# First norm in chunks, modulation on TensorE in column strips, interleaved with the first projection

## The chip, the cores and the metric

The kernel runs on one core of a Trainium2 chip. The time is the device time of one execution in microseconds. The kernel before took 2334.73 us (median of 3 runs, 2334.53 to 2340.07).

## The reference

Two blocks follow each other on 512 tokens with 1024 features, in f32. The first has two layers with a modulated norm. It also carries 256 context tokens through its first layer:

```python
sc, scc = silu(c), silu(c_ctx)
mod = split(sc @ w_mod[l] + b_mod[l], 6)       # shift1, scale1, gate1, shift2, scale2, gate2
mod_c = split(scc @ w_mod[l] + b_mod[l], 6)    # the same for the context
hn = rms_norm(h, g_norm1[l]) * (1 + mod_c[1]) + mod_c[0]
xn = rms_norm(x, g_norm1[l]) * (1 + scale1) + shift1
p = xn @ w_in[l]    # queries, keys, values; Fourier, convolution and pool inputs
```

Attention, a Fourier mixer, a convolution of width 31 with a layer norm, and a pool mixer work on p; an output projection and a SwiGLU follow. The second block has a retention layer with a short convolution and an attention layer with latent projections. The change touches only the first layer of the first block, up to its mixers.

## The kernel before

Features lie on the 128 partitions in eight chunks, tokens along the free axis: 512 of x and 256 of the context side by side, 768 in the first layer. x stays in X (`resid`) for the whole kernel.

Every large product is cut into panels of 128 output features (`panel`, L530). A panel's weights (512 KB) come into a ring of four slots. ScalarE writes their high part (`high`, L977), and VectorE (`panel_low`, L1393) or GpSimd (L523) the low part. The operand is split in the same way, and a panel step, one chunk k of the contraction, is six matmuls: high by high, low by high and high by low, each on 512 and 256 tokens. The first projection, win0, has 13 panels; `big` runs twelve one after the other, and the last stands among the mixers.

SyncE issues all loads of the ring in one written order (`ring_order`, L86). A load waits until its slot's content four places earlier has been used: a panel by `lo_ready`, a modulation block by `shift_used` or `mod_step`. The first 16 places hold the modulation blocks of shift1 (0 to 7) and scale1 (8 to 15), taken in turn. They come ahead of the first panel; x is loaded as one transfer behind the first two of them.

The shift blocks go to TensorE (L838): w is stationary and silu(c) is moving, with two columns, one for x and one for the context. The scale blocks go to VectorE (`ring_mod`, L1476; `modulate`, L1468): for each of the two vectors one multiply-and-sum pass over 128x1024. Five more blocks are done the same way right behind the first norm (L1669 to L1674), seven among the mixers (`behind`, L1761), the others later.

The first norm: ScalarE squares a chunk (L1009), GpSimd adds it to a running sum (L504). TensorE sums over partitions (L582), ScalarE takes the root (L1018), VectorE inverts (L1383) and TensorE spreads the result to all partitions (L595). For each chunk VectorE forms t = x * a * r (L1435) and ScalarE adds the shift to give the high part (L1034). The low part is VectorE's for even chunks (L1423) and GpSimd's for odd ones (L510). Panel 0 takes each chunk as it becomes ready.

In the projection VectorE makes the low parts of panels 2 to 12, the gated product for the convolution, norms and rotations of q and k, and the 62 taps of the convolution (L1684), with a table of how many have to be done at which point. The mixers (`mixers`) run ten attention pairs with other steps in between, by the table BETWEEN. The step `mean` in pair 4 sums the convolution over features on TensorE (L732) and waits for all 62 taps.

## Time and profile before

| | us |
|---|---|
| median of 3 runs | 2334.73 |
| the profiled execution | 2335.68 |
| its span | 2333.6 |
| TensorE busy (PE) | 2191.2 |
| VectorE busy (DVE) | 1211.2 |
| ScalarE busy (ACT) | 725.2 |
| GpSimd busy (POOL) | 652.0 |

Busy times come from the page's first part. PE is a matmul, PEld a load of stationary weights, and the two overlap. L544 is the line that holds every panel matmul, so where it is in time is told by the timeline. An f32 matmul outside the panels appears as two instructions, one for each of its passes. A row of the timeline merges neighbours of the same kind: start, length, engine and line, output and input, shape, count, and in brackets how long the engine stood idle before and what released it.

### The profile page before, as it was taken

The page shows a single profiled execution, that of the slowest core. Times are in us where ns is not written, and L with a number is a line of the kernel's source. Part 1 is how long each engine was busy: PE and PEld are TensorE (multiplying, and loading weights), DVE is VectorE, ACT ScalarE, POOL GpSimd, SP SyncE. Part 2 cuts the span into 40 slices and gives each one's busy share as a digit, 9 for nine tenths or more (in the row PEclk, how much of TensorE's full clock was granted, in tenths as well). Part 3 has the DMA queues.
Part 4 walks back from the last instruction along what each step waited for, and adds up shares of the span by engine and source line. Part 5 has one row for each costly group of instructions (what it writes and reads, how often), then busy time and mean ns, then how long its engine had stood idle before and what let it go on. Part 6 is the DMA issues. An engine that isn't in the chain of part 4 may idle for free.

```text
span 2333.6 us, 26283 instructions
## 1 busy us (share of the span) xinstructions
PE 2191.2 (94%) x10898; PEld 1764.2 (76%) x10898; DVE 1211.2 (52%) x1548; ACT 725.2 (31%) x1073; POOL 652.0 (28%) x283
## 2 busy tenths in 40 slices
PE   5898897999999999799989999998999999899997
PEld 5785576888888888685568888876778888778655
DVE  5996577566555665587454302346332344432265
ACT  2323433222112221424542212223253222234542
POOL 2100002223332233200044434433224444423302
PEclk9999998999999999899999999999999999989998
DMA  7312132334333333121023323322223333212301
GB/s 262 122 46 90 37 136 64 108 127 137 111 105 125 122 129 113 59 73 73 1 86 100 111 79 93 113 83 82 81 64 89 92 100 100 90 46 58 101 1 54
DMA packets 60165, 213.57 MB, mean 92 GB/s; under 512 B 6672, under 2 KB 10384, under 8 KB 59792
## 3 DMA queue, kind: packets, MB, share of 16 engines
q1 hardware_dynamic: 57888, 206.92, 27.6%
q10 hardware_dynamic: 2160, 4.98, 0.6%
q8 instruction: 87, 1.43, 0.3%
q14 instruction: 30, 0.25, 0.0%
HBM read 209.77 MB, written 2.10 MB: 91 GB/s over the span
## 4 chain that ended last, share of the span: by engine, by line
PE 85%; DVE 8%; ACT 3%; issue 2%; DMA 1%; POOL 1%; SPq 0%; ACTq 0%; DVEq 0%
PE prod L544 73%; PE misc L582 2%; PE prod L719 1%; PE prod L687 1%; DMA ring<-in_wmod 1%; PE prod L595 1%; PE prod L774 1%; ACT operand_hi L1034 1%; PE misc L903 1%; PE misc L647 1%; PE misc L798 1%; PE prod L624 1%; DVE work L1435 1%; PE misc L786 1%; DVE operand_lo L1407 1%
## 5 line engine op out<-in xcount | busy, mean ns | idle before, releaser
L523 POOL TENSOR_TENSOR wlo<-ring,whi 128x1024 fp32r<-128x1024 f32 (+3 forms) x256 | 610.4, 2385 | 1591.5 <-ACT whi L981 1591.5
L544 PE MATMUL prod<-operand_hi,whi 128*128 128x512 f32 (+1 forms) x2208 | 735.4, 373 | 36.2 <-DVE operand_lo L1423 14.1
L544 PE MATMUL prod<-operand_hi,wlo 128*128 128x512 f32 (+1 forms) x2208 | 725.1, 368 | 0.0
L544 PE MATMUL prod<-operand_lo,whi 128*128 128x512 f32 (+1 forms) x2208 | 721.3, 367 | 0.0
L981 ACT ACTIVATE whi<-ring 128x1024 fp32r<-128x1024 f32 (+3 forms) x284 | 293.5, 1034 | 736.5 <-PE prod L544 736.5
L544 PEld LDWEIGHTS prod<-operand_hi,whi 128*128 128x128 f32 x2208 | 381.8, 190 | 127.9 <-issue 28.2
L544 PEld LDWEIGHTS prod<-operand_hi,wlo 128*128 128x128 f32 x2208 | 380.6, 190 | 68.7
L544 PEld LDWEIGHTS prod<-operand_lo,whi 128*128 128x128 f32 x2208 | 379.4, 190 | 69.4 <-issue 2.4
L1473 DVE CUSTOM_DVE_ANT_0 mod_junk<-modw,silu_c,par 128x1024 bf16<-128x1024 f32 x68 | 123.7, 1820 | 79.2 <-DMA modw<-in_wmod 78.6
L544 PE MATMUL prod<-hidden_hi,whi 128*128 128x512 f32 (+1 forms) x528 | 160.6, 358 | 0.0
L544 PE MATMUL prod<-hidden_lo,whi 128*128 128x512 f32 (+1 forms) x528 | 160.4, 358 | 0.0
L544 PE MATMUL prod<-hidden_hi,wlo 128*128 128x512 f32 (+1 forms) x528 | 160.4, 358 | 0.0
L1502 DVE SCALAR_TENSOR_TENSOR resid<-prod,par,resid 128x512 f32<-128x512 f32 x72 | 45.4, 659 | 183.3 <-PE prod L544 183.2
L1799 DVE TENSOR_TENSOR hidden_lo<-ffn_h,hidden_hi 128x768 fp32r<-128x768 f32 (+1 forms) x44 | 112.5, 2556 | 42.6 <-ACT hidden_hi L1231 42.6
L1796 DVE TENSOR_TENSOR ffn_h<-ffn_silu,prod 128x768 f32<-128x768 f32 (+1 forms) x44 | 36.1, 821 | 188.0 <-PE prod L544 188.0
L1473 DVE CUSTOM_DVE_ANT_0 modw<-modw,silu_c,par 128x1024 f32<-128x1024 f32 x68 | 132.5, 1948 | 0.0
L1684 DVE SCALAR_TENSOR_TENSOR conv_acc<-glu,par,conv_acc 128x798 f32<-128x798 f32 (+1 forms) x120 | 104.4, 913 | 1.3
L1226 ACT ACTIVATE ffn_silu<-prod 128x768 f32<-128x768 f32 (+1 forms) x44 | 31.1, 706 | 224.4 <-PE prod L544 224.4
L544 PEld LDWEIGHTS prod<-hidden_hi,whi 128*128 128x128 f32 x528 | 87.1, 188 | 16.6 <-POOL wlo L523 0.5
L544 PEld LDWEIGHTS prod<-hidden_lo,whi 128*128 128x128 f32 x528 | 87.1, 188 | 16.1
L544 PEld LDWEIGHTS prod<-hidden_hi,wlo 128*128 128x128 f32 x528 | 87.1, 188 | 16.1
L1156 ACT ACTIVATE probs_t<-misc 128x512 f32<-128x512 f32 x52 | 31.0, 595 | 73.7 <-PE misc L786 73.7
(244 smaller groups left out, 2173.8 us busy)
## 6 DMA issues: line engine op xcount, KB each, us to landing
ring<-in_w SPq DMA_DIRECT2D x224, 512.0 KB, 3.6
modw<-in_wmod SPq DMA_DIRECT2D x68, 512.0 KB, 3.7
ring<-in_w SPq DMA_DIRECT2D x32, 704.0 KB, 4.9
ring<-in_wmod SPq DMA_DIRECT2D x28, 512.0 KB, 4.7
dft<-in_dftx SPq DMA_DIRECT2D x8, 512.0 KB, 5.2
resid<-in_xt SPq DMA_DIRECT2D x1, 3072.0 KB, 13.7
ring<-in_w SPq DMA_DIRECT2D x12, 192.0 KB, 2.3
ret_r<-in_decay ACTq DMA_DIRECT2D x8, 256.0 KB, 2.9
```

The lines of the kernel that those rows point to most:

```text
L523: nc.gpsimd.tensor_tensor(wlo[j % 2][:, 0:w], ring[PLACE["panel", j] % RING][:, 0:w], whi[j % 2][:, 0:w].bitcast(F32), ALU.subtract).then_ ...
L544: mm = pe.matmul(G[b][:, t0:t0 + tn], w[v][:, k * P:(k + 1) * P], a[:, t0:t0 + tn], start=(i == 0 and q == 0), stop=(i == g.kc - 1 and q = ...
L582: mm = pe.matmul(out[:, h * tb:h * tb + h], square[:, t:t + P], sel, start=(c == 0 and tb == 0), stop=(c == nchunks - 1 and tb == nb - 1), ...
L595: mm = pe.transpose(M0[:, tb * P:(tb + 1) * P], r[:, tb * P:(tb + 1) * P], ident)
L981: nc.scalar.activation(whi[j % 2][:, 0:w], ring[PLACE["panel", j] % RING][:, 0:w], ACT.Copy).then_inc(hi_ready, 1)
L1156: nc.scalar.activation(probs_t[at % 3][:, :], M1[:, :], ACT.Copy).then_inc(pair_copied, 1)
L1226: nc.scalar.activation(fsilu[:, 0:width], src[:, 0:width], ACT.Silu).then_inc(free, 1)
L1473: nc.vector.tensor_tensor_reduce((junk, w)[s][:, 0:DC * P], w[:, 0:DC * P], silu_c[:, 1024 * s:1024 * (s + 1)], 1.0, col, ALU.mult, ALU.ad ...
L1502: ins = nc.vector.scalar_tensor_tensor(X[:, p, t0:t0 + tn], G[b][:, t0:t0 + tn], pa(f"mod{l}")[:, col:col + 1], X[:, p, t0:t0 + tn], ALU.m ...
L1684: ins = nc.vector.scalar_tensor_tensor(o, glu[:, c, tap:tap + wide], w, o, ALU.mult, ALU.add)
L1796: nc.vector.tensor_tensor(fh[:, 0:width], fsilu[:, 0:width], G[b][:, 0:width], ALU.mult).then_inc(bank_free[b], 1)
L1799: nc.vector.tensor_tensor(HL[:, p // 2, 0:width], fh[:, 0:width], HH[:, p // 2, 0:width].bitcast(F32), ALU.subtract).then_inc(h_lo, 1)
```

## The change

- Parameters, constants and x come first. Constants are issued on ScalarE's queue, x in four transfers with a semaphore each; c for VectorE's products comes behind the load of panel 3.
- ScalarE squares each chunk as its quarter lands; VectorE adds the squares instead of GpSimd.
- All 16 blocks of shift1 and scale1 go to TensorE, with silu(c) as the stationary operand, padded with zeros from 2 to 32 columns, and w as the moving one. The eight contraction chunks of a block go in turn to four column strips of 32, so that eight matmuls leave four partial sums in rows 0 to 127. ScalarE copies the rows of a chunk out (`mod_copy`), and TensorE multiplies them with a 0/1 matrix (`pick`), which adds the four partial sums and puts features back on partitions. VectorE adds the bias and forms the factor for that chunk alone (`mod_chunk`) ahead of its t.
- On TensorE the sum of squares comes first, then the chunks of modulation, from chunk 4 on between the steps of panels 0 and 1. These two run side by side, panel 1 one step behind. Modulation runs four chunks ahead.
- On ScalarE the high parts of panels 0 and 1 stand ahead of the copies of chunks 1 and 2.
- The ring holds six blocks, panels 0 and 1, ten blocks, panels 2 and 3, and then blocks 16 to 20 in turn with panels 4 to 8.
- Blocks 16 to 20 are multiplied on VectorE between the low parts of panels 2 to 7 instead of behind the norm. Fifty instead of 62 convolution taps lie in the projection; the other twelve stand in pairs 0, 2, 3 and 4 of the mixers (`beside`).

The buffers for the padded vector and the copied rows lie in space that is free then; new semaphores are declared. The diff without these:

```diff
-MOD_PE = 8
-MOD_FIRST = 16
+MOD_PE = 16
...
     panels = [("panel", j) for g in GEMMS for j in range(g.j0, g.j0 + g.n)]
-    first = [("mod", k // 2 + MOD_PE * (1 - k % 2)) for k in range(MOD_FIRST)]
-    order = first + panels[:2]
-    for i in range(4):
-        order += [("mod", MOD_FIRST + k) for k in ((0, 1), (2,), (3,), (4,))[i]] + [panels[2 + i]]
+    first = [("mod", k // 2 + DC * (1 - k % 2)) for k in range(MOD_PE)]
+    order = first[:6] + panels[:2] + first[6:] + panels[2:4]
+    for i in range(5):
+        order += [("mod", MOD_PE + i), panels[4 + i]]
     cut = GEMM["wout0"].j0 + 2
-    return order + panels[6:cut] + [("mod", k) for k in range(MOD_FIRST + 5, MOD_RING)] + panels[cut:]
+    return order + panels[9:cut] + [("mod", k) for k in range(MOD_PE + 5, MOD_RING)] + panels[cut:]
...
     for name, w in (("ident", 128), ("ones", 128), ("perm1", 128), ("perm2", 128), ("mask", 128),
-                    ("invw", 2), ("edge", 32), ("inv", 1), ("eps", 1), ("half", 2)):
+                    ("invw", 2), ("edge", 32), ("inv", 1), ("eps", 1), ("half", 2), ("pick", 2)):
...
         def _(sp):
-            sp.dma_start(silu_c[:, :], d["c"]).then_inc(c_landed, 16)
             sp.dma_start(par[:, :], d["par"]).then_inc(par_landed, 16)
-            sp.dma_start(con[:, :], d["con"]).then_inc(par_landed, 16)
+            for s in range(4):
+                sp.dma_start(X[:, 2 * s:2 * s + 2, :], d["xt"][:, 2 * s:2 * s + 2, :]).then_inc(x_landed[s], 16)
...
                 elif i < MOD_PE:
-                    sp.wait_ge(shift_used, i + 1)
+                    sp.wait_ge(shift_used, 2 * (i % DC) + 2 - i // DC)
...
-            for r in range(RING // 2):
-                load_mod(ORDER[r][1])
-            sp.dma_start(X[:, :, :], d["xt"]).then_inc(x_landed, 16)
             own = MOD_RING
-            for kind, j in ORDER[RING // 2:]:
+            for kind, j in ORDER:
...
                 load_panel(j)
+                if j == 3:
+                    sp.dma_start(silu_c[:, :], d["c"]).then_inc(c_landed, 16)
...
         def _(pool):
-            for c in range(1, DC):
-                pool.wait_ge(square_ready, c + 1)
-                wait(pool, square_added, c - 1)
-                nc.gpsimd.tensor_tensor(W[1][:, :], W[1][:, :], W[0][:, :], ALU.add).then_inc(square_added, 1)
             def odd_lows(name):
...
-            pe.wait_ge(c_ready, 1)
-            for k in range(MOD_PE):
-                landed(pe, ("mod", k))
-                w = ring[PLACE["mod", k] % RING]
-                for c in range(DC):
-                    mm = pe.matmul(M0[:, 2 * k:2 * k + 2], w[:, c * P:(c + 1) * P], silu_cp[:, 2 * c:2 * c + 2],
-                                   start=(c == 0), stop=(c == DC - 1))
-                mm.then_inc(shift_used, 1)
+            def modulate(c):
+                bank = (M1, MM)[c % 2]
+                wait(pe, mod_read, c - 1)
+                for q in (1, 0):
+                    landed(pe, ("mod", DC * q + c))
+                    w = ring[PLACE["mod", DC * q + c] % RING]
+                    for i in range(DC):
+                        g = 32 * (i % 4)
+                        mm = pe.matmul(bank[g:g + 32, P * q:P * q + P], silu_cp[:, 32 * i:32 * i + 32], w[:, i * P:(i + 1) * P],
+                                       start=(i < 4), stop=(i >= 4))
+                    mm.then_inc(shift_used, 1)
+            def pick(c):
+                pe.wait_ge(mod_copied, c + 1)
+                for q in range(2):
+                    mm = pe.matmul((M1, MM)[c % 2][:, 256 + 2 * q:258 + 2 * q], mod_rows[c % 2][:, P * q:P * q + P], co("pick"),
+                                   start=True, stop=True)
+                mm.then_inc(mod_picked, 1)
+            def first_panels(p, k):
+                def ready(k):
+                    if k % 2:
+                        pe.wait_ge(odd_lo, k // 2 + 1)
+                    else:
+                        pe.wait_ge(operand_lo, k + 1)
+                panel("win0", p, xh, xl, NT, k, k + 1, ready=ready)
+            pe.wait_ge(con_landed, 16)
+            sum_squares(1, NT, W, total=W[1], out=F[:, 0:8])
+            pe.wait_ge(pad_ready, 1)
+            modulate(0)
+            modulate(1)
+            pick(0)
+            spread_roots(NT, W)
+            modulate(2)
+            pick(1)
+            modulate(3)
+            pick(2)
+            for k in range(DC + 1):
+                if k < DC:
+                    first_panels(0, k)
+                if k + 3 < DC:
+                    pick(k + 3)
+                if k:
+                    first_panels(1, k - 1)
+                if k + 4 < DC:
+                    modulate(k + 4)
...
                 width, segs = tok(l)
-                if l == 0:
-                    rms(1, NT, W, free=lambda: pe.wait_ge(shift_read, 1), total=W[1])
-                else:
+                if l == 1:
...
-                big(f"win{l}", xh, xl, lambda p, l=l: win_width(l, p), ready=OPS[f"win{l}"], after=qk_norm, panels=12)
+                big(f"win{l}", xh, xl, lambda p, l=l: win_width(l, p), ready=OPS[f"win{l}"], after=qk_norm, panels=12,
+                    begin=0 if l else 2)
...
+            def mod_copy(c):
+                act.wait_ge(shift_used, 2 * c + 2)
+                wait(act, mod_picked, c - 1)
+                nc.scalar.activation(mod_rows[c % 2][:, :], (M1, MM)[c % 2][:, 0:256], ACT.Copy).then_inc(mod_copied, 1)
             def norm_mod(l, which, width):
-                root(width, 1024)
-                if l == 0 and which == 0:
+                first = l == 0 and which == 0
+                root(width, 1024, source=F[:, 0:8] if first else None)
+                if first:
+                    mod_copy(0)
                     high(0)
+                    mod_copy(1)
                     high(1)
+                    mod_copy(2)
...
+                    if first and 0 < c < DC - 2:
+                        mod_copy(c + 2)
...
-            act.wait_ge(par_landed, 32)
-            nc.scalar.activation(silu_cp[:, :], pa("c"), ACT.Silu)
-            act.wait_ge(c_landed, 16)
-            nc.scalar.activation(silu_c[:, :], silu_c[:, :], ACT.Silu).then_inc(c_ready, 1)
-            act.wait_ge(x_landed, 16)
+            act.dma_start(con[:, :], d["con"]).then_inc(con_landed, 16)
+            act.wait_ge(par_landed, 16)
+            act.wait_ge(pad_cleared, 1)
+            nc.scalar.activation(silu_cp[:, :].rearrange("p (c s) -> p c s", c=DC)[:, :, 0:2],
+                                 pa("c").rearrange("p (c s) -> p c s", c=DC), ACT.Silu).then_inc(pad_ready, 1)
+            for c in range(DC):
+                act.wait_ge(x_landed[c // 2], 16)
+                wait(act, square_added, c - 2)
+                nc.scalar.activation((W[4 + c % 2] if c else W[1])[:, :], X[:, c, 0:NT], ACT.Square).then_inc(square_ready, 1)
+            n["added"] += DC - 1
+            n["sq"] += 1
+            act.wait_ge(con_landed, 16)
...
                 width, segs = tok(l)
-                if l == 0:
-                    for c in range(DC):
-                        square(c, X[:, c, 0:NT], NT, W[0], W[1], lambda c: None)
                 norm_mod(l, 0, NT)
...
                 def qk_norm(p, l=l):
+                    if l == 0 and p == 1:
+                        act.wait_ge(c_landed, 16)
+                        nc.scalar.activation(silu_c[:, :], silu_c[:, :], ACT.Silu).then_inc(c_ready, 1)
...
-            def norm_mod(l, which, width):
+            def mod_chunk(c):
+                both = pa("mod0")[:, 0:4 * DC].rearrange("p (b c s) -> p c b s", b=2, c=DC)[:, c]
+                dve.wait_ge(mod_picked, c + 1)
+                nc.vector.tensor_tensor(both, both, (M1, MM)[c % 2][:, 256:260].rearrange("p (b s) -> p b s", b=2),
+                                        ALU.add).then_inc(mod_read, 1)
+                dve.wait_ge(mod_read, c + 1)
+                link(nc.vector.tensor_scalar(afac[:, c:c + DC + 1:DC], both[:, 1], 1.0, pa("g10")[:, c:c + 1], ALU.add, ALU.mult))
+            def norm_mod(l, which, width, before=None):
...
                 for c in range(DC):
+                    if before is not None:
+                        before(c)
...
-            dve.wait_ge(par_landed, 32)
-            dve.wait_ge(c_ready, 1)
-            for k in range(MOD_PE, MOD_FIRST):
-                ring_mod(k)
-            dve.wait_ge(shift_used, MOD_PE)
-            shift = pa("mod0")[:, 0:2 * MOD_PE]
-            nc.vector.tensor_tensor(shift, shift, M0[:, 0:2 * MOD_PE], ALU.add).then_inc(shift_read, 1)
-            dve.wait_ge(shift_read, 1)
-            dve.wait_ge(mod_step, mods_done(MOD_FIRST - 1))
+            nc.vector.memset(silu_cp[:, :], 0.0).then_inc(pad_cleared, 1)
+            dve.wait_ge(par_landed, 16)
+            for c in range(1, DC):
+                dve.wait_ge(square_ready, c + 1)
+                wait(dve, square_added, c - 1)
+                nc.vector.tensor_tensor(W[1][:, :], W[1][:, :], W[4 + c % 2][:, :], ALU.add).then_inc(square_added, 1)
...
             n["added"] += DC - 1
-            modulation(0, 0)
-            dve.wait_ge(x_landed, 16)
+            for s in range(4):
+                dve.wait_ge(x_landed[s], 16)
...
                 width, segs = tok(l)
-                norm_mod(l, 0, NT)
+                norm_mod(l, 0, NT, mod_chunk if l == 0 else None)
...
                 link(ins)
-                if l == 0:
-                    for k in range(MOD_FIRST, MOD_FIRST + 3):
-                        ring_mod(k)
                 panel_low(g.j0 + 2)
-                if l == 0:
-                    for k in range(MOD_FIRST + 3, MOD_FIRST + 5):
-                        ring_mod(k)
                 dwa, dwba, ticks = PAR[f"dw{l}"][0], PAR[f"dwb{l}"][0], {}
...
                     panel_low(g.j0 + 3 + 2 * c)
-                    conv_taps(((7, 20), (5, 12))[l][c])
+                    if l == 0 and c == 0:
+                        dve.wait_ge(c_ready, 1)
+                    if l == 0:
+                        ring_mod(MOD_PE + 2 * c)
+                    conv_taps(((5, 16), (5, 12))[l][c])
                     panel_low(g.j0 + 4 + 2 * c)
-                    conv_taps(((13, 26), (10, 18))[l][c])
+                    if l == 0:
+                        ring_mod(MOD_PE + 2 * c + 1)
+                    conv_taps(((9, 21), (10, 18))[l][c])
...
                     panel_low(g.j0 + p + 2)
+                    if l == 0 and p == 5:
+                        ring_mod(MOD_PE + 4)
...
                         rope(PR[:, p - 5, 0:NX], W[4][:, 0:NX])
-                    conv_taps(((33, 39, 45, 51, 57, 62), (25, 35, 45, 53, 57, 62))[l][p - 5])
+                    conv_taps(((25, 30, 35, 40, 45, 50), (25, 35, 45, 53, 57, 62))[l][p - 5])
...
                         pooling(c, part)
+                    if l == 0 and i < 5:
+                        conv_taps((52, 52, 54, 58, 62)[i])
...
                     if l == 0 and i in (0, 3, 4, 5, 6, 7, 8):
-                        ring_mod(MOD_FIRST + 5 + (0, 3, 4, 5, 6, 7, 8).index(i))
+                        ring_mod(MOD_PE + 5 + (0, 3, 4, 5, 6, 7, 8).index(i))
...
     put("eps", EPS)
+    put("pick", i[:, None] % 32 == np.arange(2)[None, :])
...
```

## Rows read from the trace of the kernel before

**Rows 1.** The page, part 1, the whole span: busy us, share, instructions.

```profile
PE 2191.2 (94%) x10898; PEld 1764.2 (76%) x10898; DVE 1211.2 (52%) x1548; ACT 725.2 (31%) x1073; POOL 652.0 (28%) x283
```

**Rows 2.** Windows: stretch, its length, each engine's busy us (x instructions), granted clock, DMA.

```profile
0.00:61.23 61.23, 32.35 (x146) 31.49 (x147) 35.42 (x44) 16.43 (x21) 18.30 (x13) 1.00 0.72 259
61.23:84.69 23.46, 20.14 (x88) 16.43 (x89) 22.72 (x46) 12.71 (x22) 7.80 (x4) 0.93 0.44 134
84.69:182.68 97.99, 97.99 (x578) 84.58 (x576) 90.67 (x105) 21.86 (x28) 0.00 (x0) 1.00 0.20 62
```

**Rows 3.** The chain of waits in the start: start us, length us, what.

```profile
44.60 6.98 PE prod L838 x32
```

**Rows 4.** Timeline of TensorE from the sum of squares into panel 0.

```profile
51.44 2.70 PE L582 MATMUL misc<-con,work 128*128 128x1 f32 x12
55.41 1.54 PE L595 MATMUL prod<-con,work 128*128 128x128 f32 x6 [1.27 <-DVE work L1384]
61.23 0.98 PE L544 MATMUL prod<-operand_hi,whi 128*128 128x512 f32 x2 [4.28 <-DVE operand_lo L1423]
...
63.32 1.01 PE L544 MATMUL prod<-operand_hi,whi 128*128 128x512 f32 x2
...
79.74 0.51 PE L544 MATMUL prod<-operand_hi,whi 128*128 128x512 f32 x2
...
80.80 0.51 PE L544 MATMUL prod<-operand_hi,whi 128*128 128x512 f32 x2
```

**Rows 5.** DMA up to 17.16 us: packets and rate; then KB each, us to landing.

```profile
DMA packets 955, 6.20 MB, mean 361 GB/s; under 512 B 96, under 2 KB 224, under 8 KB 699
...
resid<-in_xt SPq DMA_DIRECT2D x1, 3072.0 KB, 13.7
```

**Rows 6.** DMA up to 100 us, one modulation block of the ring.

```profile
ring<-in_wmod SPq DMA_DIRECT2D x21, 512.0 KB, 4.6
```

**Rows 7.** Timeline of all engines: first squares, operands of panel 0, behind panel 0.

```profile
17.16 1.58 ACT L1009 ACTIVATE work<-resid 128x768 f32<-128x768 f32 x2 [7.86 <-DMA resid<-in_xt]
...
51.62 0.17 DVE L1647 TENSOR_TENSOR par<-par,prod 128x16 f32<-128x16 f32 x1 [3.18 <-PE prod L838]
...
56.99 2.19 DVE L1435 SCALAR_TENSOR_TENSOR work<-resid,afac,prod 128x512 f32<-128x512 f32 x4 [1.63 <-PE prod L595]
58.17 2.17 ACT L1034 ACTIVATE operand_hi<-work,par 128x512 fp32r<-128x512 f32 x4 [1.83 <-DVE work L1435]
59.32 1.76 DVE L1423 SCALAR_TENSOR_TENSOR operand_lo<-work,par,operand_hi 128x512 fp32r<-128x512 f32 x2
...
61.43 1.84 POOL L510 TENSOR_TENSOR operand_lo<-work,operand_hi 128x768 fp32r<-128x768 f32 x1 [1.28 <-ACT work L1034]
...
76.29 0.81 ACT L1181 ACTIVATE conv_acc<-prod 128x768 f32<-128x768 f32 x1 [2.50 <-PE prod L544]
...
77.00 1.05 ACT L981 ACTIVATE whi<-ring 128x1024 fp32r<-128x1024 f32 x1
...
81.16 1.22 DVE L1397 TENSOR_TENSOR wlo<-ring,whi 128x1024 fp32r<-128x1024 f32 x1
```

**Rows 8.** Groups of instructions by shape, VectorE's adds of squares: count | busy, mean ns.

```profile
L1375 DVE TENSOR_TENSOR work<-work,work 128x768 f32<-128x768 f32 x7 | 6.7, 954 | 1.0 <-ACT work L1009 1.0
```

**Rows 9.** Timeline, one weighing of V, two strips of 64 columns, two narrow windows.

```profile
218.97 0.39 PE L798 MATMUL misc<-probs_t,vtok 128*64 128x128 f32 x4
...
219.08 0.28 PE L798 MATMUL misc<-probs_t,vtok 128*64 128x128 f32 x2
```

**Rows 10.** Timeline of VectorE: taps in the projection, mixers.

```profile
92.77 6.48 DVE L1684 SCALAR_TENSOR_TENSOR conv_acc<-glu,par,conv_acc 128x798 f32<-128x798 f32 x6
...
207.94 1.28 DVE L1473 CUSTOM_DVE_ANT_0 mod_junk<-ring,silu_c,par 128x1024 bf16<-128x1024 f32 x1 [12.14 <-issue]
...
250.64 0.68 DVE L1407 TENSOR_TENSOR operand_lo<-misc,operand_hi 128x512 fp32r<-128x512 f32 x1
```

**Rows 11.** Timeline of TensorE in pair 4: the layer norm's mean.

```profile
252.05 2.95 PE L732 MATMUL prod<-conv_acc,con 128*128 128x512 f32 x8
```

9 lines of the change are left out of this document (6 added, 3 removed).

## The prediction

> **What bounds the kernel now.** I read the page's busy times first: TensorE is busy for 94% of the span [rows 1], so a gain has to come from the places where it stands still or runs slowly. The windows show where one lies. Up to 61.23 us TensorE is busy for 32.35 us, none of it on a projection, and from 61.23 to 84.69 for 20.14 of 23.46 us. From 84.69 to 182.68 it is busy for all 97.99 us [rows 2]. Panel 1 of the first projection ends at 84.69, so everything ahead of that point is the start. The chain of waits names what holds the start: the last two shift blocks on TensorE end at 51.6 us [rows 3], behind 16 block loads of which eight wait for VectorE's two multiply-and-sum passes. Only then come the sum of squares (2.70 us), the spread of the roots (1.54 us) and, at 61.23 us, the first projection matmul [rows 4]. A step of a panel (six matmuls) starts every 2.09 us there and every 1.06 us from 79.74 us on [rows 4]: TensorE's lower (1.2 GHz) and its upper level (2.4 GHz).
>
> **What goes, comes and moves.** I time the new start on TensorE up to the point that answers to 84.69 us.
>
> *Squares.* Parameters and constants (0.6 MB by their widths) and x (3072 KB, [rows 5]) now come first, 3.7 MB. In the first 17.16 us 6.20 MB came in, 361 GB/s on average [rows 5], so the last quarter of x lands near 11 us instead of 17. A square takes ScalarE some 0.84 us for a chunk [rows 7] and an add on VectorE 0.95 us [rows 8]; the seven adds run behind the landings and end near 14.0 us (bounds 13 and 16). GpSimd's adds go. Sum of squares, at the lower level, 2.7 us: 16.8 us.
>
> *Modulation of one chunk.* Two blocks, each eight matmuls with 32 stationary and 128 moving columns in f32, that is two passes each, 32 passes a chunk. No row has four strips. The nearest is the weighing of V in two strips of 64 columns: two passes start inside each 0.11 us at the upper level (four passes from 218.97, the last two from 219.08) [rows 9]. Four strips at once would be 8 slots of 0.11, 0.9 us a chunk. No overlap would be 32 passes, 3.5 us. Two at a time, as in the row, would be 1.8. I take 1.3 us, between four and two at a time, and twice that, 2.6 us, at the lower level. The Trainium skill (TensorE: Matmul & The Clock Gate, Part 3, "The mechanism") says that a weight load overlaps running matmuls only where the row groups differ, and here all strips use all rows. By that rule each load would stand between matmuls and a chunk would cost at least the 3.5 us. The two strips of this trace share all rows too and do run together, so I keep this as a rival.
>
> *Pick.* Four passes against 128-column weights at 0.225 us (2.70 us for 12 in rows 4): 0.9 us low, 0.4 high. The ACT copy ahead of it, 128x256, is a third of a chunk's high part (2.17 us for two chunks, [rows 7]), so under 0.5 us, and lies beside the next chunk's matmuls. It costs nothing while that next chunk is there; without cover it would be 0.5 us for each.
>
> *Order on TensorE.* Chunks 0 and 1, pick, spread: 16.8 + 5.2 + 0.9 + 1.5 = 24.4 us. Chunk 2: 27.0. The blocks of chunk 3 may load only as chunk 2's ring slots come free, the second at 27.0, and a load takes 4.6 us [rows 6]: its last half starts at 31.6, chunk 3 ends at 32.9, pick 2 at 33.8. By then panels 0 and 1 have landed and been split (their loads start near 21 us, and high parts stand ahead of the copies on ScalarE), and VectorE and ScalarE have chunks 0 and 1 ready: t takes VectorE 1.1 us a chunk, the high part ScalarE 1.1, the low part 1.2 to 1.8 [rows 7]. The new wait for a pick stands ahead of each t on VectorE; behind it wait t, then ScalarE's high part, then GpSimd's odd low part. Its two tiny instructions are near the 0.17 us of the shift add [rows 7], 0.45 us a chunk with the handshake. Four steps pass: k=0 still low, 2.1 + 0.9 + 2.6 = 5.6 us; k=1 to 3 high, two panel steps, pick and chunk, 2.1 + 0.4 + 1.3 = 3.8 us each. That is 50.8 us. VectorE and ScalarE need about 2.2 us a chunk for operands and are ahead. Step k=4 and pick 7 end at 52.3. From there chunk 7's own chain ends last: 0.45 + 1.1 + 2.2 (ScalarE writes high part and a copy) + 1.84 (GpSimd's low part) = 5.6 us, then three panel steps, 3.2 us: 61.1 us.
>
> *Panel 2.* Before, its low part lay ready while panel 1 ran for 8.5 us. Now panel 1 ends 2.1 us after panel 0, and sigmoid 0.81, high part 1.05 and low part 1.22 [rows 7] take 3.1 us: a new stall of 1.0 us. Panel 2 starts at 62.1 instead of 84.69. **Gain of the start: 22.6 us.**
>
> *VectorE behind it.* Five block products (two passes of 1.28 us, [rows 10]) leave the end of the start and go between panels 2 to 7; twelve conv taps of 1.08 us (6.48 us for six, [rows 10]) leave the projection for the mixers. The sums are equal (12.8 and 13.0 us) and VectorE is busy 90.67 of 97.99 us there [rows 2], with an earlier beginning now, so TensorE stays covered; for a low part that comes a little late at panel 6 or 7 I put 0.5 us (0 to 5). Two of the twelve taps stand before the 12.14 us wait for a modulation load [rows 10] and cost nothing. Two and four in front of pairs 3 and 4's norms shift these by some 1.3 us, which a running TensorE hides. The last four do not hide: they start when VectorE has finished a low part at 250.64 + 0.68 = 251.32 us [rows 10] and end at 255.65, while TensorE now starts the layer norm's mean, which needs all taps, at 252.05 [rows 11]. **Loss: 3.6 us** (0 if TensorE has a reserve there, 5 if the shift before it adds up). The silu of c moves behind panel 1's evacuation, where ScalarE is busy 21.86 of 97.99 us [rows 2]: nothing.
>
> *Sum.* -22.6 + 0.5 + 3.6 = -18.5 us. The profiled execution took 2335.68 us (span 2333.6), so 2317.2; it lies 0.95 us above the median of 2334.73, so the forecast is **2316 us**.
>
> **The rivals.**
> 1. *Strips run in full parallel and the mean's wait is hidden.* A chunk at 0.9/1.8 us brings panel 2 to 58 us or so, and the 3.6 us stay out: 2309 us. For it: the two strips of rows 9 overlap completely. Against: weight loads of four strips in 0.11 us are seen nowhere. 0.20.
> 2. *TensorE stays at its lower level through the interleaved steps.* k=1 to 3 then cost 4.2 + 0.9 + 2.6 = 7.7 us each and the end 4.6 us more, panel 2 starts near 78.4: 2335.7 - 6.3 + 4.1, by the median 2332 us. For it: before 61 us TensorE ran its block matmuls seven us without a gap and its sum of squares still at 0.225 us a pass [rows 3, 4]. Against: the same trace is at the upper level by 79.74, with the steps that now make half of the mix. 0.12.
> 3. *Slower: strips one after another.* Place: TensorE's modulation; price 3.5 us a chunk high and 7.0 low. Chunk 3 then ends at 23.8 + 24.5 = 48.3, the steps at 77.2 and panel 2 starts at 88.5, 3.8 later than now, with the mixers' 4.1: 2343 us, and with the clock low throughout 2365. It decides from 5.7 us for a cold chunk (each extra us there counts six times: 3.5 chunks ahead, one in k=0, three halves). That is where the skill's rule on weight loads leads. Rows 9 speak against it. 0.08.
> 4. *VectorE becomes the bound of the projection.* With 5 more us of late low parts there and 1 or 2 in the mixers: 2323 us. For it: 93% busy in rows 2, and a product that waits for its block holds every low part behind it. Against: the sum of its work doesn't grow. 0.10.
>
> **How the numbers follow.** My forecast, 2311 to 2323 in itself, has 0.50. Differences within 0.3% (7 us) can't be told from none. Faster: the forecast, rivals 1 and 4, 0.80. Same: rival 2, 0.12. Slower: rival 3, 0.08. The range goes from rival 1 to just under rival 2: 2308 to 2331 us, which leaves out about 0.2.
>
> **What would show it.** Right: first projection matmul near 34 us; panel 2's first near 62; four modulation passes started in some 0.15 us at the upper level; squares' last add at 14 us; TensorE without a gap from panel 2 to the mixers; the wait before the mean (line 732's instructions) named after conv taps, about 3.6 us. Wrong: a modulation chunk over 3.2 us, matmuls of panel steps still 0.43 us apart after 45 us, loads for chunks 3 to 7 landing after the previous step has ended, or low parts of panels 4 to 8 named as what TensorE waits for.

## The result

| | median, us | runs | ratio to before |
|---|---|---|---|
| kernel before | 2334.73 (2334.53 to 2340.22) | 5 | |
| changed kernel | 2319.53 (2315.53 to 2321.93) | 5 | 0.9924 [0.9908, 0.9941] |

The change made the kernel 15.2 us faster by the medians. The forecast was 2316 us, 3.5 us lower, and its range (2308 to 2331) held the time. The profiled execution of the changed kernel took 2319.09 us, its span 2317.3 us.

### The profile page after: what moved, and what is told of

Read it like the earlier page. It is cut to its first block, busy times and chain, and to the rows that moved or that the text cites. A ratio compares the mean times of both kernels' runs of the same rounds, so it can differ in the third digit from the quotient of the medians.

```text
span 2317.3 us, 26618 instructions
## 1 busy us (share of the span) xinstructions
PE 2182.1 (94%) x11058; PEld 1753.8 (76%) x11058; DVE 1189.9 (51%) x1537; ACT 730.3 (32%) x1083; POOL 637.0 (27%) x276
## 4 chain that ended last, share of the span: by engine, by line
PE 86%; DVE 7%; ACT 3%; issue 1%; DMA 1%; POOL 1%; SPq 0%; ACTq 0%; DVEq 0%
PE prod L542 74%; PE misc L580 2%; PE prod L717 1%; PE prod L685 1%; PE prod L772 1%; DMA ring<-in_wmod 1%; DVE conv_acc L1742 1%; PE misc L941 1%; PE misc L645 1%; PE prod L593 1%; PE misc L796 1%; PE prod L622 1%; PE misc L784 1%; DVE operand_lo L1463 1%; PE misc L613 1%
## 5 line engine op out<-in xcount | busy, mean ns | idle before, releaser
L1742 DVE SCALAR_TENSOR_TENSOR conv_acc<-glu,par,conv_acc 128x798 f32<-128x798 f32 (+1 forms) x120 | 104.6, 914 | 1.3
L542 PEld LDWEIGHTS prod<-hidden_hi,whi 128*128 128x128 f32 x528 | 87.2, 188 | 16.3 <-POOL wlo L521 0.5
```

The source lines that it names most:

```text
L542: mm = pe.matmul(G[b][:, t0:t0 + tn], w[v][:, k * P:(k + 1) * P], a[:, t0:t0 + tn], start=(i == 0 and q == 0), stop=(i == g.kc - 1 and q = ...
L1742: ins = nc.vector.scalar_tensor_tensor(o, glu[:, c, tap:tap + wide], w, o, ALU.mult, ALU.add)
```

## The profile after

The page's first part, engine by engine: busy us, share of the span, instructions. It answers to [rows 1].

```profile
PE 2182.1 (94%) x11058; PEld 1753.8 (76%) x11058; DVE 1189.9 (51%) x1537; ACT 730.3 (32%) x1083; POOL 637.0 (27%) x276
```

TensorE's busy time fell by 9.1 us while the span fell by 16.3: part of the gain is work that ran at the higher clock level or went away, the rest is standing time.

The windows of the changed kernel, in the columns of [rows 2]. I cut at events: first panel matmul, panel 2's first, the end of attention's first scores, the mean, the last scores of layer 0.

```profile
0.00:34.57 34.57, 13.25 (x158) 10.77 (x159) 13.51 (x21) 15.88 (x24) 5.07 (x7) 0.86 0.76 276
34.57:62.25 27.68, 26.16 (x244) 21.82 (x244) 15.17 (x44) 14.96 (x27) 7.17 (x4) 0.92 0.80 295
...
157.75:231.38 73.63, 59.10 (x329) 37.75 (x329) 47.34 (x88) 29.53 (x60) 4.75 (x2) 0.92 0.22 79
231.38:281.19 49.81, 41.74 (x217) 26.32 (x218) 29.97 (x55) 23.92 (x36) 0.00 (x0) 0.84 0.17 48
```

The same cuts in the kernel before, by its own events:

```profile
86.10:182.61 96.51, 96.51 (x569) 83.29 (x567) 90.50 (x103) 21.86 (x28) 0.00 (x0) 1.00 0.19 58
182.61:252.05 69.44, 58.58 (x329) 37.47 (x328) 36.25 (x77) 28.78 (x59) 4.76 (x2) 0.95 0.23 84
252.05:297.66 45.61, 37.53 (x220) 23.57 (x218) 29.98 (x55) 24.68 (x38) 0.00 (x0) 0.93 0.17 52
```

Laid side by side, in us:

| stretch | before | after | difference |
|---|---|---|---|
| start to panel 2's first matmul | 86.10 | 62.25 | -23.85 |
| panel 2 to the first scores | 96.51 | 95.50 | -1.0 |
| first scores to the mean | 69.44 | 73.63 | +4.2 |
| mean to the last scores of layer 0 | 45.61 | 49.81 | +4.2 |
| everything behind | 2036.0 | 2036.1 | +0.1 |
| span | 2333.6 | 2317.3 | -16.3 |

So the start gained 23.85 us and the mixers gave back 8.4. In the fourth row TensorE is *busy* 4.2 us longer with the same matmuls, and the granted clock is 0.84 where it was 0.93: that half of the loss is no standing time at all.

The timeline of TensorE in the changed kernel shows the start and the two places in the mixers (start, length, what, and in brackets the idle time before and its releaser):

```profile
15.79 2.69 PE L580 MATMUL prod<-con,work 128*128 128x1 f32 x12 [15.79 <-DVE work L1713]
18.41 3.54 PE L840 MATMUL misc<-ring,silu_c_by_feature 128*32 128x128 f32 x64
...
25.97 1.08 PE L840 MATMUL misc<-ring,silu_c_by_feature 128*32 128x128 f32 x16 [1.87 <-DMA ring<-in_wmod]
...
28.72 1.01 PE L848 MATMUL misc<-con,mod_rows 128*128 128x2 f32 x4 [1.68 <-ACT mod_rows L1063]
...
31.36 2.22 PE L840 MATMUL misc<-ring,silu_c_by_feature 128*32 128x128 f32 x32 [1.62 <-DMA ring<-in_wmod]
...
34.57 0.98 PE L542 MATMUL prod<-operand_hi,whi 128*128 128x512 f32 x2
...
39.06 0.62 PE L542 MATMUL prod<-operand_hi,whi 128*128 128x512 f32 x2
...
41.80 1.08 PE L840 MATMUL misc<-ring,silu_c_by_feature 128*32 128x128 f32 x32
...
62.25 0.61 PE L542 MATMUL prod<-operand_hi,whi 128*128 128x512 f32 x2 [1.06 <-DVE wlo L1453]
...
231.38 5.58 PE L730 MATMUL prod<-conv_acc,con 128*128 128x512 f32 x8 [3.56 <-DVE conv_acc L1742]
...
247.96 5.28 PE L580 MATMUL prod<-con,glu 128*128 128x1 f32 x24
```

Three things are to be seen. A modulation chunk (32 passes, L840) takes 1.08 us at the upper level (41.80). At the lower one it takes 1.77 us where two stand in a row (half of 3.54, 18.41) and 2.22 us behind a wait (31.36). Ahead of the first panel matmul TensorE waits 1.87 + 1.68 + 1.62 = 5.2 us for blocks and for one copy. And the mean's eight matmuls, 2.95 us in [rows 11], take 5.58 behind the 3.56 us wait for the taps; the 24 passes of the next sum of squares, 17 us later, take 5.28. In the kernel before they take 3.71:

```profile
265.56 3.71 PE L582 MATMUL prod<-con,glu 128*128 128x1 f32 x24
```

That is 2.63 + 1.57 = 4.2 us, the whole of the table's fourth row. The two parts are of different kinds. The mean runs at the upper level in the kernel before. The sum of squares is in part at the lower level there too: the windows of these 24 passes, before and after, have a granted clock (the number behind the five engines) of 0.74 and 0.50.

```profile
265.56:269.13 3.57, 3.57 (x27) 3.57 (x25) 0.00 (x0) 0.00 (x0) 0.00 (x0) 0.74 0.02 5
```
```profile
247.96:253.10 5.14, 5.14 (x27) 5.14 (x25) 0.00 (x0) 0.00 (x0) 0.00 (x0) 0.50 0.02 3
```

VectorE and ScalarE in the changed kernel, start and mixers, where the adds, squares and late taps are:

```profile
9.38 6.27 DVE L1713 TENSOR_TENSOR work<-work,work 128x768 f32<-128x768 f32 x6 [0.23 <-ACT work L1219]
...
6.51 1.57 ACT L1219 ACTIVATE work<-resid 128x768 f32<-128x768 f32 x2 [1.91 <-DMA resid<-in_xt]
...
13.62 0.84 ACT L1219 ACTIVATE work<-resid 128x768 f32<-128x768 f32 x1 [0.22 <-DVE work L1713]
...
226.93 4.30 DVE L1742 SCALAR_TENSOR_TENSOR conv_acc<-glu,par,conv_acc 128x798 f32<-128x798 f32 x4
```

The adds end at 15.65. The last square (13.62) waits for an add and not for x. The four taps before the mean are one solid row: 1.08 us each with nothing between, as in [rows 10].

## Experiments

Eleven kernels ran, each an edit of the changed kernel. The line labels in the rows are those of each kernel. Landmarks from the traces, in us:

| kernel | first panel matmul | panel 2 | first scores | mean starts | its 8 matmuls | last scores |
|---|---|---|---|---|---|---|
| before | 61.23 | 86.10 | 182.61 | 252.05 | 2.95 | 297.66 |
| changed | 34.57 | 62.25 | 157.75 | 231.38 | 5.58 | 281.19 |
| e1 | 34.12 | 61.97 | 158.10 | 229.66 | 4.61 | 278.13 |
| e2 | 34.00 | 61.82 | 161.96 | 231.59 | 2.95 | 277.19 |
| e3 | 40.32 | 71.33 | 166.82 | 238.87 | 5.01 | 287.82 |
| e4 | 40.76 | 78.23 | 174.36 | 247.60 | 5.59 | 297.42 |
| e5 | 39.11 | 68.75 | 164.24 | 237.28 | 5.35 | 286.76 |
| e6 | 50.68 | 70.90 | 167.04 | 240.88 | 5.66 | 290.78 |
| e7 | 39.15 | 66.88 | 162.38 | 236.04 | 5.59 | 285.86 |
| e8 | 35.98 | 65.88 | 162.02 | 234.97 | 5.24 | 284.27 |
| e9 | 34.01 | 61.43 | 156.93 | 219.38 | 2.95 | 266.54 |
| e10 | 34.25 | 64.00 | 160.13 | 233.00 | 2.95 | 278.59 |
| e11 | 34.84 | 62.29 | 157.79 | 222.61 | 4.64 | 271.13 |

What lies behind the last scores (the start of layer 0's last two score matmuls) takes 2031.8 to 2039.5 us from trace to trace, though only e9 and e11 change anything there, the places of a few block products. Landmarks are therefore compared with landmarks, times with times. The kernel before had a median of 2333.85 us beside e1 to e4, 2337.19 beside e5 to e8 and 2336.0 beside e9 to e11; ratios are to these.

### e1_taps_pair0: the twelve late taps in front of the wait for a block

```diff
-                        conv_taps((52, 52, 54, 58, 62)[i])
+                        conv_taps((60, 60, 60, 60, 62)[i])
```

> The changed kernel with ten of the twelve moved taps in pair 0, where VectorE stands still for its modulation block, two in pair 4, none in pairs 2 and 3. Theory W (the taps ahead of the mean cost the wait and TensorE's clock behind it): the 3.6 us wait of the mean falls to under 2 us, the mean's matmuls take 2.95 us again instead of 5.58 and the 24 passes of the norm's squares 3.7 instead of 5.3; 5 to 8 us off, a time of 2311 to 2314 us. Rival F (the wait only takes the place of a later one): the wait goes, but under 2 us come off, 2318 us or more.

2317.10 us, ratio 0.9925 [0.9907, 0.9944]. The timeline of TensorE:

```profile
229.66 4.61 PE L730 MATMUL prod<-conv_acc,con 128*128 128x512 f32 x8 [1.38 <-DVE conv_acc L1742]
```

The wait shrank from 3.56 to 1.38 us, but the matmuls behind it still ran slow, and the mean to the last scores took 48.47 us against 49.81. So theory W was right on the wait and wrong on the clock: 2.95 us had been expected for the mean, and 5 to 8 us off. The landmark came 3.1 us earlier; in the time nothing can be told from the changed kernel's 0.9924.

### e2_taps_projection: all 62 taps in the projection again

```diff
-                    conv_taps(((5, 16), (5, 12))[l][c])
+                    conv_taps(((7, 20), (5, 12))[l][c])
-                    conv_taps(((9, 21), (10, 18))[l][c])
+                    conv_taps(((13, 26), (10, 18))[l][c])
-                    conv_taps(((25, 30, 35, 40, 45, 50), ...)[l][p - 5])
+                    conv_taps(((33, 39, 45, 51, 57, 62), ...)[l][p - 5])
-                        conv_taps((52, 52, 54, 58, 62)[i])
+                        conv_taps(62)
```

> All 62 taps in the projection again, with the five block products beside them. Theory V (VectorE has 7 us of room there, 88.4 busy of 95.5 us): 13 us more taps overrun it by 6 us or so, TensorE waits for low parts or norms of q and k, the mean's wait and its low clock go (8 us); 2315 to 2321 us, with the gain of one eaten by the other. Rival: VectorE's idle time there absorbs them, 2311 us.

2316.04 us, ratio 0.9919 [0.9898, 0.994]. The timeline of TensorE, then the window of the projection:

```profile
109.32 0.87 PE L593 MATMUL prod<-con,work 128*128 128x128 f32 x6 [2.48 <-DVE work L1440]
...
111.13 0.84 PE L542 MATMUL prod<-operand_hi,wlo 128*128 128x512 f32 x2
...
231.59 2.95 PE L730 MATMUL prod<-conv_acc,con 128*128 128x512 f32 x8
...
245.10 3.79 PE L580 MATMUL prod<-con,glu 128*128 128x1 f32 x24
```

```profile
61.82:161.96 100.14, 97.65 (x566) 84.44 (x566) 97.79 (x118) 25.30 (x31) 0.00 (x0) 0.98 0.25 74
```

With no wait ahead of the mean both rows are back, at 2.95 and 3.79 us, and the stretch from the mean to the last scores is 45.6 us, as before. Here VectorE is what the projection waits for: it is busy 97.79 of the projection's 100.14 us, and that stretch is 4.6 us longer than with fifty taps. TensorE stands 2.5 us for the inverted roots (L593), and the two panel steps behind this wait take 1.83 and 1.90 us instead of 1.06, with panel matmuls at the lower level (0.84 us for two at 111.13). From the first scores to the last scores e2 takes 115.2 us against 123.4. So the twelve taps cost some 8 us behind the projection or 4.6 inside it, but the last scores come only 4.0 us sooner, and the times don't differ measurably. The result lies in the range that theory V gave.

### e3_pool_adds: the adds of squares on GpSimd

```diff
-            for c in range(1, DC):                 # VectorE
-                ...
-                nc.vector.tensor_tensor(W[1], W[1], W[4 + c % 2], ALU.add)
+            for c in range(1, DC):                 # GpSimd
+                ...
+                nc.gpsimd.tensor_tensor(W[1], W[1], W[4 + c % 2], ALU.add)
```

> The seven adds of squares on GpSimd again, all else as changed. Theory P (the sum of squares stands at the head of the path): an add with its handshake takes 2.76 us instead of 1.06, the last ends near 27 instead of 15.7, panel 2 starts 8 to 11 us later, 2328 to 2331 us. Rival D (block loads set the start, the sum is hidden): under 3 us more.

2324.78 us, ratio 0.996 [0.9945, 0.9975]. The timeline of GpSimd and TensorE:

```profile
8.18 13.47 POOL L507 TENSOR_TENSOR work<-work,work 128x768 f32<-128x768 f32 x7 [7.74 <-ACT work L1224]
...
21.80 2.69 PE L585 MATMUL prod<-con,work 128*128 128x1 f32 x12 [21.80 <-POOL work L507]
...
45.82 0.84 PE L547 MATMUL prod<-operand_lo,whi 128*128 128x512 f32 x2
```

An add takes GpSimd 13.47 / 7 = 1.92 us against 1.05 on VectorE. The sum of squares starts 6.0 us later, panel 2 9.1: the other 3 us are panel steps that are still at the lower level at 45.82 (0.84 us for two matmuls; 0.62 at 39.06 in the changed kernel). The adds are on the path, and having them on VectorE is worth 5 us by the medians, 8 by the ratios. Panel 2's delay lies in the 8 to 11 us of theory P; the time lies 3 us below what it gave.

### e4_one_strip: the same modulation in one column strip

```diff
-                        g = 32 * (i % 4)
+                        g = 0
-                                       start=(i < 4), stop=(i >= 4))
+                                       start=(i == 0), stop=(i == DC - 1))
```

with the copy and the pick on rows 0 to 31 alone.

> All eight matmuls of a modulation block in the same 32 columns, summed in PSUM; the copy and the pick take 32 rows. Theory S (four strips run at once): a chunk costs 3.5 us high and 7 low instead of 0.95 and 1.75; panel 2 starts 20 to 29 us later, 2339 to 2349 us. Rival (the loads of weights, not the matmuls, set a chunk's time): under 5 us more, 2324 us or less.

2332.95 us, ratio 0.9989 [0.9974, 1.0004]. The timeline of TensorE:

```profile
18.35 10.06 PE L840 MATMUL misc<-ring,silu_c_by_feature 128*32 128x128 f32 x64
...
49.19 3.68 PE L840 MATMUL misc<-ring,silu_c_by_feature 128*32 128x128 f32 x32
```

The same 32 passes cost 3.68 us in one strip and 1.08 in four, a factor of 3.4. By the Trainium skill (TensorE: Matmul & The Clock Gate, Part 3, "The mechanism") a weight load overlaps running matmuls only where the row groups differ; all four strips use all rows, and yet they overlap. Without the strips nearly the whole gain is gone. It is a smaller loss than the third rival had, and than the 20 to 29 us that theory S had expected here, since panel 2 comes 16.0 us later: the solid matmuls of the first two chunks take 10.06 us and not 14, so they reached the upper level on their way.

### e5_x_whole: x as one transfer

```diff
-            for s in range(4):
-                sp.dma_start(X[:, 2*s:2*s+2, :], d["xt"][:, 2*s:2*s+2, :]).then_inc(x_landed[s], 16)
+            sp.dma_start(X[:, :, :], d["xt"]).then_inc(x_landed[0], 16)
```

> The changed kernel with x in one transfer. Theory P (the squares stand at the head of the path): the squares start near 11.5 instead of 6.5, the last add ends near 20 instead of 15.7, panel 2 starts 3 to 4.5 us later: 3 to 4.5 us longer than the changed kernel. Rival D (loads of blocks set the start): under 1 us longer.

2323.35 us, ratio 0.9943 [0.9928, 0.9958]. The timeline of ScalarE and VectorE:

```profile
11.75 2.31 ACT L1218 ACTIVATE work<-resid 128x768 f32<-128x768 f32 x3 [7.30 <-DMA resid<-in_xt]
...
13.43 7.33 DVE L1712 TENSOR_TENSOR work<-work,work 128x768 f32<-128x768 f32 x7 [12.30 <-ACT work L1218]
```

The squares begin at 11.75 instead of 6.51, the adds end at 20.76 instead of 15.65, and panel 2 comes 6.5 us later, where 3 to 4.5 had been expected. By medians and by ratios the quarters are worth about 4 us, but the two intervals overlap; the landmarks show the difference, the times alone do not.

### e6_modulation_first: all chunks of modulation ahead of the panels

```diff
+            for k in range(4, DC):
+                modulate(k)
+                pick(k - 1)
+            pick(DC - 1)
             for k in range(DC + 1):
-                if k + 3 < DC:
-                    pick(k + 3)
-                if k + 4 < DC:
-                    modulate(k + 4)
```

> All eight chunks of modulation on TensorE first, then the steps of panels 0 and 1 side by side. Theory I (lying among the panel steps hides the modulation's loads): TensorE waits for the blocks of chunks 4 to 7, all picked near 46 us, then 16 steps of 1.05 us; panel 2 starts near 65 instead of 62.3, 3 us longer than the changed kernel. Rival (chunk 7's chain ends last in either order): within 1 us.

2325.18 us, ratio 0.9949 [0.9931, 0.9967]. The timeline of TensorE:

```profile
47.94 1.08 PE L840 MATMUL misc<-ring,silu_c_by_feature 128*32 128x128 f32 x16 [0.88 <-DMA ring<-in_wmod]
...
50.68 0.99 PE L542 MATMUL prod<-operand_hi,whi 128*128 128x512 f32 x2
```

Chunks 4 and 7 wait for their blocks, four times and 4.3 us in all, and the passes between stay at the lower level: 16 in 1.08 us. Panel 2 comes 8.65 us later; I had put it at 3. So panel steps between the chunks do fill the time of the loads. How much of the 8.65 us is these waits and how much the lower level, this run doesn't part.

### e7_ring_eight_copies_first and e8_copies_first: ring order, and copies ahead of high parts

```diff
-    order = first[:6] + panels[:2] + first[6:] + panels[2:4]
+    order = first[:8] + panels[:2] + first[8:] + panels[2:4]        # e7 only
```
```diff
                     mod_copy(0)
-                    high(0)
                     mod_copy(1)
-                    high(1)
                     mod_copy(2)
+                    high(0)
+                    high(1)                                          # e7 and e8
```

> Eight blocks in the ring ahead of panels 0 and 1 instead of six, and the copies of chunks 0 to 2 ahead of the high parts. Theory L (in the changed kernel TensorE waits for the second blocks of chunks 2 and 3 and for a copy behind a high part, 5.2 us in all): the waits for chunk 3 and for copy 1 go, but panel 0's split now ends last; first projection matmul between 34 and 36 us, against 34.6: within 2 us of the changed kernel. Rival: the splits of panels 0 and 1 have reserve, and 2 to 4 us come off.

> The copies of chunks 0 to 2 ahead of the high parts of panels 0 and 1, all else as changed. Theory L: the 1.7 us wait for copy 1 behind high part 0 goes, but the blocks of chunk 3 land no sooner, so the first projection matmul stays within 0.5 us of 34.6 and the time within 1 us of the changed kernel. Rival: pick 1 comes 1.7 us sooner, and so does everything behind it, 1.5 us off.

e7: 2321.25 us, ratio 0.9932 [0.9915, 0.995]. e8: 2319.89 us, ratio 0.993 [0.991, 0.995]. The timeline of TensorE in e7:

```profile
39.15 0.98 PE L542 MATMUL prod<-operand_hi,whi 128*128 128x512 f32 x2 [9.71 <-DVE operand_lo L1488]
```

and in e8:

```profile
23.48 0.64 PE L840 MATMUL misc<-ring,silu_c_by_feature 128*32 128x128 f32 x16 [0.46 <-DMA ring<-in_wmod]
...
31.67 2.23 PE L840 MATMUL misc<-ring,silu_c_by_feature 128*32 128x128 f32 x32 [5.06 <-DMA ring<-in_wmod]
...
35.98 0.98 PE L542 MATMUL prod<-operand_hi,whi 128*128 128x512 f32 x2 [1.13 <-DVE operand_lo L1488]
...
41.48 0.84 PE L542 MATMUL prod<-operand_lo,whi 128*128 128x512 f32 x2
```

With the panels two places later in the ring, e7's first panel matmul waits 9.7 us and comes at 39.15, not between 34 and 36 as expected. In e8 TensorE waits 5.06 us for chunk 3's block in one piece, where the changed kernel waits 1.62 at that place and 1.7 for a copy earlier, so what the earlier copies save there is lost again to the load. Ahead of the wait e8 is at the upper level (16 passes in 0.64 us at 23.48; the changed kernel is too at that point), behind it at the lower one (32 in 2.23), and its panel steps still are at 41.48. Its first panel matmul comes 1.4 us later, where within 0.5 had been expected, and panel 2 is 3.6 us later. Neither time can be told from the changed kernel's: the order of copies and high parts, and the two places in the ring, were not shown to matter.

### e9_no_product_in_pair0: no block product ahead of pair 1

The longest wait in the changed kernel's mixers is not the mean's. Its waits between 157 and 232 us (what waits <- for what: us, times, longest):

```profile
PE misc L784 <- DVE work L1687: 7.2, 1, 7.2
```

L784 turns a pair's probabilities, which needs a norm of VectorE's; VectorE stands in pair 0's block product. The kernel before waits 12.14 us there ([rows 10]), for nothing that the row names; the changed kernel's timeline names the block's load:

```profile
183.18 1.28 DVE L1540 CUSTOM_DVE_ANT_0 mod_junk<-ring,silu_c,par 128x1024 bf16<-128x1024 f32 x1 [10.06 <-DMA ring<-in_wmod]
```

The kernel before has that product there too, and TensorE waits 7.1 us behind it.

```diff
-                        conv_taps((52, 52, 54, 58, 62)[i])
+                        conv_taps((57, 59, 60, 62, 62)[i])
-                    if l == 0 and i in (0, 3, 4, 5, 6, 7, 8):
-                        ring_mod(MOD_PE + 5 + (0, 3, 4, 5, 6, 7, 8).index(i))
+                    if l == 0 and i > 2:
+                        ring_mod(MOD_PE + 2 + i)
```

> The seven block products of the mixers behind pairs 3 to 9 instead of 0 and 3 to 8; taps up to 57, 59, 60, 62 behind pairs 0 to 3. Theory Q (VectorE's wait for a block behind the DFT tables holds pair 1's norm): the 7.2 us wait of TensorE in pair 1 goes or shrinks to the DFT tables' landing, and so do the mean's 3.6 us and the low clock behind it: 9 to 15 us off the changed kernel. Rival (the tables themselves land late): the wait moves to the DFT matmuls of pair 2, and only the mean's 5 to 8 us come off.

**2306.18 us**, ratio 0.9877 [0.9862, 0.9893]. The waits of that stretch, and the timeline of TensorE:

```profile
PE misc L784 <- DVE work L1687: 2.8, 2, 2.0
```

```profile
219.38 2.95 PE L730 MATMUL prod<-conv_acc,con 128*128 128x512 f32 x8
...
233.35 5.28 PE L580 MATMUL prod<-con,glu 128*128 128x1 f32 x24
```

The window from the first scores to the mean:

```profile
156.93:219.38 62.45, 56.64 (x329) 35.89 (x328) 47.05 (x84) 28.64 (x59) 5.59 (x2) 1.00 0.23 85
```

The wait of 7.2 is down to 2.0 at most, and from the first scores to the mean it takes 62.45 us, against 73.63 in the changed kernel and 69.44 before. Of the 11.2 us against the changed kernel, 8.7 are standing time. The other 2.5 are the same 329 matmuls, which are busy 56.64 us at a granted clock of 1.00 and were busy 59.10 at 0.92. This kernel beats both others: its interval lies wholly below the changed kernel's. One thing does not follow theory Q: with no wait ahead of the mean, which runs in 2.95 us, the sum of squares behind it still takes 5.28 us, as in the changed kernel. The two edits ran together here; e10 and e11 part them.

### e10_taps_spread and e11_spread_no_product

e10: nine more taps in the projection at spread points, three in pair 0, pair 0's product kept. e11: the same with e9's products.

```diff
-                    conv_taps(((25, 30, 35, 40, 45, 50), ...)[l][p - 5])
+                    conv_taps(((27, 33, 39, 46, 53, 59), ...)[l][p - 5])
-                        conv_taps((52, 52, 54, 58, 62)[i])
+                        conv_taps(62)
```

> 59 taps in the projection, most of the added ones behind panel 7 on, and the last three in pair 0's wait. Theory W: no wait for taps at the mean, which runs at the upper level (2.95 us), no wait for the inverted roots at panel 6 (2.5 us with all taps in the projection): 7 to 9 us off the changed kernel in the trace. Rival F (something else ends as late): under 3 us.

> Both: taps up to 59 in the projection and 62 in pair 0, and no block product before pair 3. If both theories hold the gains add: 14 to 17 us off the changed kernel, near 2303 us. Rival: with the product gone the three taps in pair 0 delay its next norms, and the sum comes to under 10 us.

e10: 2316.67 us, ratio 0.9919 [0.9903, 0.9934]. e11: 2306.99 us, ratio 0.9876 [0.986, 0.9892]. The waits of e10 between 160 and 235 us:

```profile
PE misc L784 <- DVE work L1687: 7.0, 1, 7.0
PE prod L772 <- ACT work L1187: 2.1, 1, 2.1
```

and the timeline of e11:

```profile
222.61 4.64 PE L730 MATMUL prod<-conv_acc,con 128*128 128x512 f32 x8
```

Freed of its wait for taps, e10 keeps the 7.0 us wait, and a new one of 2.1 us appears for ScalarE in pair 0 (L772 <- L1187), which e11 has too. e10's time can't be told from the changed kernel's, e11's not from e9's. So the products are what counts: between e10 and e11 their places alone differ (none behind pair 0, one behind pair 9, the others as they come), and the medians lie 9.7 us apart. The gains did not add as I had expected: e11 was to come near 2303 us. Where the taps stand is worth no time that can be measured. In the trace e10 does gain: from the first scores to the last it takes 118.5 us against 123.4. But its start took 1.75 us longer to panel 2 and its projection 0.6, with the same code as the changed kernel in the start.

The mean's row in e11 is also the exception to what e1 and e2 suggest. Its mean waits for nothing and still takes 4.64 us. In the last 5 us ahead of it TensorE is busy exactly as long as in e10, where the mean takes 2.95 us; the windows of these 5 us, of e11 and then of e10:

```profile
217.61:222.61 5.00, 3.25 (x24) 1.83 (x24) 2.73 (x5) 3.05 (x7) 0.00 (x0) 1.00 0.00 0
```
```profile
228.00:233.00 5.00, 3.25 (x24) 1.83 (x25) 2.73 (x5) 3.05 (x7) 0.00 (x0) 1.00 0.00 0
```

## Why the prediction came out, step by step

- **The start, forecast 22.6 us, measured 23.85.** Panel 2 was forecast at 62.1 and came at 62.25. I had the other end wrong: I read panel 1's end as 84.69, which lies inside one of its steps. The window by events puts panel 2 of the kernel before at 86.10. The working was right for the place it was made for, and the difference is 1.4 us too small for a boundary read too early. The prediction also names only 79.74 as the point from which the steps are fast. The timeline of the kernel before has them at the upper level from 66.00 to 76.09 already, and then slow again for 3.6 us behind a wait:

```profile
74.92 0.62 PE L544 MATMUL prod<-operand_hi,whi 128*128 128x512 f32 x2 [1.83 <-POOL operand_lo L510]
...
77.95 0.84 PE L544 MATMUL prod<-operand_hi,whi 128*128 128x512 f32 x2
```

So the slow matmuls behind a wait, which the forecast left out at the mean, stood in the trace that it was made from.
- **Inside the start, errors cancelled.** The adds ended at 15.65, not 14.0: six of them are a chain of 6.27 us from 9.38, 1.05 us each and not 0.95, and the last square waits for an add, not for x. A chunk of modulation costs 1.08 us high and 1.77 to 2.22 low, not 1.3 and 2.6, so the chunk terms were each dearer than they are. But 5.2 us of waits for blocks and a copy stood among the first four chunks, where I had one wait of 3.3 us for the load of chunk 3. The first panel matmul was forecast at 33.8 and came at 34.57. That the two ends agree so well is in part luck.
- **The clock in the steps (rival 2).** The upper level was reached by 39.06 us, in the k=1 step, as assumed. In e3 and e8 the same steps were still at the lower level at 45.82 and at 41.48 us, and panel 2 came 3.3 and 2.2 us later than the delay of the first panel matmul explains. So a rise late by some steps is real, but costs 2 to 3 us and not the 16 of a clock that stays low throughout. Part of it is chance: e1, e2, e9, e10 and e11 have the changed kernel's code up to panel 2, and panel 2 comes between 61.43 and 64.00 us; e10, the latest, has two matmuls in 0.84 us still at 40.40.
- **The strips (rivals 1 and 3).** Four strips run nearly at once, and without them (e4) the change would be worth nothing that can be measured: 0.9989. Rival 1's price of a chunk (0.9 and 1.8 us) was nearer than mine, but its panel 2 at 58 us left out the waits of the start. Rival 3's price was right for one strip at the upper level (3.68 us), its 2343 us too high by 10.
- **Panel 2's new stall**, forecast 1.0 us, measured 1.06, for the low part.
- **VectorE in the projection**, forecast +0.5 us, measured -1.0. With fifty taps no low part behind panel 2 comes late, so the term is 0. The -1.0 isn't VectorE's: TensorE is busy throughout in both kernels, but most panel steps start every 1.04 us (at 70.68 and 71.72) where they were 1.06 apart. Why is open; e1, with the same projection, took 96.13 us for it and not 95.50. Rival 4 did not happen; e2 shows that it would with all 62 taps, for 4.6 us.
- **The mean's wait**, forecast 3.6 us, measured 3.56, ended by the taps at L1742. Named right, sized right, and still the place of the largest miss: I had priced only the standing time. Behind it the same matmuls cost another 4.2 us: the mean +2.6, the sum of squares +1.6. For the mean the wait is the likely cause. All eight kernels with a wait ahead of it (the changed one, e1, e3 to e8) take 4.61 to 5.66 us. Of the five without one, four take 2.95 (before, e2, e9, e10) and e11 takes 4.64. The wait goes with the low clock, then, but it isn't needed for it. For the sum of squares it isn't shown: e9 and e11 have no wait ahead of the mean and take the same 5.28 us, while before, e2 and e10 take 3.71 to 4.09. These 1.6 us stay open.
- **The sum.** Forecast -22.6 + 0.5 + 3.6 = -18.5. Measured in the profiled executions -23.85 - 1.0 + 4.2 + 4.2 + 0.1 = -16.3. The error is 2.2 us: the unpriced clock +4.2, the start -1.25, the projection -1.5, and +0.6 between the first scores and the mean. The windows place that last term: TensorE stands 14.53 us there against 10.86, which is the 3.56 us wait and 0.1 more, and the same 329 matmuls are busy 0.5 us longer at a granted clock of 0.92 against 0.95. So 4.7 us of slow matmuls were left out, and 2.75 us of other misses hid more than half of them. The forecast's number is better than its terms.

The step that the prediction lacked is thus the clock behind the new wait: it had the mean's matmuls at 2.95 us and they took 5.58. What stays open is when exactly the level changes: panel steps had the upper one by 39.06 us in one trace and not at 40 to 46 in others, e10 with the same start among them, and e11's mean and e9's sum of squares were slow without a wait ahead of the mean. No run isolates that.

## What to carry to other kernels

A wait of a few microseconds in front of dense TensorE work has to be priced twice: once for the wait, and once for matmuls behind it at the lower clock. Here the mean cost 2.6 us more behind a wait of 3.56 us, and 1.7 more behind one of 1.38. A trace of the kernel before can already show such places. Runs of the same code in one stretch moved a landmark by up to 2.6 us (panel 2), so a difference of that size in one trace proves nothing. Small-output f32 matmuls put in four column strips run 3.4 times as fast as in one, if the partial sums can be added by a later small matmul. After a change to an order, read the longest wait of the new trace, wherever it is: here VectorE stood in the product of a block that had not landed, and TensorE waited 7 us for VectorE. Moving the products was worth 9.7 us, more than half of the whole change, and the wait was in the kernel before already.

## What the runs showed of the hardware

- Four column strips of 32 that use the same rows overlap: 32 f32 passes of 128 columns take 1.08 us at the upper level, 3.68 in one strip.
- A wait of 1.38 us before the mean (e1) was followed by eight matmuls in 4.61 us instead of 2.95, one of 3.56 us by 5.58 us; e11 took 4.64 with no wait. In e2 two panel steps behind a wait of 2.48 us took 1.83 and 1.90 us instead of 1.06. In e8, 16 passes took 0.64 us ahead of a wait of 5.06 us and 32 took 2.23 behind it.
- The sum of squares behind the mean had a granted clock of 0.74 before and 0.50 in the changed kernel: 24 passes in 3.71 and 5.28 us. It took 5.28 in e9 too, where nothing waited ahead of the mean.
- An add of 128x768 f32 takes 1.92 us a piece on GpSimd and 1.05 on VectorE (6.27 us for six), both with two buffers in turn.
- The level of the clock in the first panel steps differs between traces, even where the code up to there is the same (upper from 39.06 us in the changed kernel, still lower at 40.40 in e10), and moves panel 2 by 2 to 3 us.
